# Convolution and layer-norm phase order by way of DRAM, Toeplitz weights on GpSimd, and a third GLU block among the x loads

## The reference

```python
u = glu[..., :D_CONV] * jax.nn.sigmoid(glu[..., D_CONV:])      # 1024 channels
uc = jnp.concatenate([u_past, u], axis=1)
y = lax.conv_general_dilated(uc, w_dw[:, None, :], ...) + b_dw  # depthwise, 31 taps along the sequence
y = jax.nn.silu(layer_norm(y, ln_g, ln_b))                      # over the 1024 channels
conv_out = y @ w_pw + b_pw
```

## Time and profile before

| | |
|---|---|
| median of 3 runs | 2202.6 us (2202.15 to 2210.67) |
| profiled execution, device time | 2203.41 us |
| its span, slowest core (6) | 2201.9 us; all cores 2185.9 to 2201.9 |
| TensorE busy | 2026.9 us, 92% |
| VectorE, ScalarE, GpSimd busy | 740.7, 441.7, 133.4 us |
| DMA, mean | 106 GB/s |

### The profile page before, as it was taken

How to read it: one execution, slowest core, us unless ns; L and a number is a source line. 1 busy time by engine, 2 the same in 40 slices (tenths; PEclk the granted TensorE clock), 3 DMA queues, 4 the chain that set the end, 5 groups by cost and what they waited for, 6 DMA issues and landing times.

```text
span 2201.9 us, 35215 instructions; the slowest of 8 cores (2185.9 to 2201.9 us)
## 1 busy us (share of the span) xinstructions
PE 2026.9 (92%) x13348; PEld 1266.4 (58%) x13348; DVE 740.7 (34%) x1185; ACT 441.7 (20%) x814; POOL 133.4 (6%) x253
## 2 busy tenths in 40 slices
PE   4667876499999999999999999999999999999997
PEld 3445543266555456666678865565565665655653
DVE  3445553222232232222223414414324224234126
ACT  4323434333222331111102310000000000000113
POOL 0000005500000000000000000000000000000000
PEclk9778777799999999999999999999999999999999
DMA  9244343323966868796374455584674643542423
GB/s 242 45 106 89 89 76 77 65 76 92 156 130 126 138 112 188 114 179 120 62 140 118 77 101 100 93 153 85 107 139 84 108 91 70 98 82 47 89 41 153
DMA packets 58459, 234.42 MB, mean 106 GB/s; under 512 B 13773, under 2 KB 32317, under 8 KB 43037
## 3 DMA queue, kind: packets, MB, share of 16 engines
q0 software_dynamic: 32080, 139.94, 38.1%
q1 hardware_dynamic: 26214, 92.23, 15.1%
HBM read 349.99 MB, written 59.99 MB: 186 GB/s over the span
## 4 chain that ended last, share of the span: by engine, by line
PE 84%; DMA 5%; DVE 3%; ACT 3%; issue 2%; POOL 2%; SPq 1%; DVEq 0%; ACTq 0%; POOLq 0%
PE ps L125 84%; DVE arena L125 3%; DMA arena<-xext 3%; ACT arena L125 2%; DMA arena<-arena 2%; POOL arena L142 2%; SPq L142 1%; ACT L125 0%; DMA y<-arena 0%; DVEq L85 0%; ACTq L85 0%; SPq L85 0%; POOLq L85 0%
## 5 line engine op out<-in xcount | busy, mean ns | idle before, releaser
L125 PE MATMUL ps<-arena 128*128 128x512 bf16 (+10 forms) x13348 | 2026.9, 320 | 161.4 <-DVE arena L125 122.7
L125 PEld LDWEIGHTS ps<-arena 128*128 128x128 bf16 (+2 forms) x13348 | 1266.4, 102 | 921.5 <-issue 206.9
L125 DVE TENSOR_TENSOR arena<-ps,arena 128x512 f32<-128x512 f32 (+5 forms) x729 | 412.7, 569 | 966.2 <-PE ps L125 710.5
L125 ACT ACTIVATE arena<-ps 128x348 f32<-128x348 f32 (+3 forms) x284 | 132.4, 476 | 1073.3 <-PE ps L125 1072.0
L125 ACT ACTIVATE arena<-arena 128x1 f32<-128x1 f32 (+7 forms) x183 | 124.1, 689 | 251.1 <-DVE arena L125 193.5
L125 DVE TENSOR_TENSOR arena<-arena 128x128 bf16<-128x128 f32 (+10 forms) x219 | 144.0, 661 | 36.4 <-ACT arena L125 18.2
L125 DVE SCALAR_TENSOR_TENSOR arena<-ps,arena 128x348 f32<-128x348 f32 (+4 forms) x74 | 46.7, 631 | 293.4 <-PE ps L125 291.1
L125 ACT COPY arena<-ps 128x512 bf16<-128x512 bf16 (+7 forms) x151 | 91.7, 621 | 129.8 <-PE ps L125 112.5
L125 DVE SCALAR_TENSOR_TENSOR arena<-arena 128x2048 bf16<-128x2048 f32 (+5 forms) x36 | 79.2, 2201 | 74.8 <-ACT arena L125 68.7
L125 ACT CAST arena<-ps 128x384 bf16<-128x384 f32 x72 | 36.9, 513 | 183.0 <-PE ps L125 181.4
L142 POOL DMA_DIRECT2D arena<-arena x128 | 63.3, 499 | 39.6 <-ACT arena L125 35.5
(11 more groups left out here) (18 smaller groups left out, 44.7 us busy)
## 6 DMA issues: line engine op xcount, KB each, us to landing
arena<-wgu POOLq DMA_DIRECT2D x44, 1024.0 KB, 8.3
arena<-wgate POOLq DMA_DIRECT2D x16, 1408.0 KB, 18.2
arena<-w_down POOLq DMA_DIRECT2D x11, 2048.0 KB, 27.1
arena<-xext SPq DMA_DIRECT2D x19, 1024.0 KB
arena<-wqkv POOLq DMA_DIRECT2D x9, 2048.0 KB, 17.8
kso<-ck SPq DMA_DIRECT2D x16, 1022.0 KB
vso<-cv SPq DMA_DIRECT2D x16, 1022.0 KB
arena<-wglu POOLq DMA_DIRECT2D x8, 1024.0 KB, 11.5
```

The costliest lines, as they stand in the source:

```text
L125: self.q[eng].append(lambda e, meth=meth, a=a, kw=kw, s=s: getattr(e, meth)(*a, **kw).then_inc(s, 1))
```

## The change

1. `glu_end` writes its block to a DRAM tensor `u_scr` with one DMA and reads it back in the other order with four, one for each f. They stay on SyncE's queue; the reads wait for the write.
2. The Toeplitz builds leave `glu_end` and VectorE: `tbuild(n)` does them on GpSimd, for blocks 0 and 1 in `consts`, for n + 2 at the end of `conv(n)`, each q with a key of its own.
3. `ln_n` is split in `ln_norm` and `ln_silu`. The Silu writes bf16 over its own fp32 operand; one DMA writes the block to `c_scr` in DRAM and four read it into `cT`, all on SyncE's queue instead of GpSimd's. `ln_step` does the norm of block i and the Silu of block i - 1, at steps 4 to 7 and twice at each of k and v steps 0 and 1, once at 2.
4. Blocks 0, 1 and 2 of GLU run among the first tiles, one third of one block behind a tile. A fourth weight slot and a third `uph` buffer come with it. Halo tiles 0 and 1 are loaded at tile 2. `conv(0)` follows directly.
5. In the loop over blocks 3 to 7 the norm of the next halo tile is issued right behind the transposes of the last one, and `conv(n - 1)` stands between the second and the last third of block n.
6. Weight loads move with the slots: GLU 4 and 5 behind `conv(0)`, GLU 6 and the q weights behind block 4, GLU 7 behind block 5, and the k weights in halves behind blocks 6 and 7.
7. `conv_last` moves from step 0 to step 1, `ln_sample` to 2 and `ln_mean` to 3; in group 2 the sample projection moves from k and v step 1 to 2.

```diff
+    u_d = nc.dram_tensor("u_scr", [8, 128, 1056], BF16, kind="Internal").ap()
+    c_d = nc.dram_tensor("c_scr", [8, 128, 1024], BF16, kind="Internal").ap()
...
-        GLUW = (0, 2048, 8192)
+        GLUW = (0, 2048, 8192, 10240)
+        GLUS = (0, 1, 2, 3, 0, 1, 0, 1)
...
+        after('pool', XBK[4])
+        glu_load(2)
...
         def glu_end(n):
-            for q in range(4):
-                for f in range(4):
-                    S.dma('sp', uP[ui][32 * f:32 * f + 32, q, :], uph[ui][32 * q:32 * q + 32, f, :], reads=[pk], writes=['%s_%d%d' % (Pk, q, f)])
+            S.dma('sp', u_d[n], uph[hi][:, :, :].rearrange("p f m -> p (f m)"), reads=[pk], writes=['ud%d' % n])
+            for f in range(4):
+                S.dma('sp', uP[ui][32 * f:32 * f + 32, :, :], u_d[n].rearrange("(q c) (f m) -> f c q m", q=4, f=4)[f], reads=['ud%d' % n], writes=['%s_%d' % (Pk, f)])
...
+        def tbuild(n):
             w4n = w4[:, 144 * n:144 * n + 144]
             for q in range(4):
-                S.op('dve', lambda e: e.tensor_tensor(out=v3(tpw[ui][q], 36), ...
+                S.op('pool', lambda e: e.tensor_tensor(out=v3(tpw[n % 2][q], 36), ...
...
-        GLU_AT = {2: 0, 5: 1, 9: 2}
+        GLU_AT = {2: ((0, 0),), 3: ((1, 0),), 5: ((0, 1),), 6: ((1, 1),), 7: ((2, 0),), 8: ((2, 1),), 9: ((0, 2), (1, 2), (2, 2))}
...
+            for n, part in GLU_AT.get(ti, ()):
+                glu(n, part)
+                if part == 2 and n < 2:
+                    glu_end(n)
+                    conv_out(n)
+        conv(0)
+        glu_end(2)
+        glu_load(4)
+        glu_load(5)
...
+        def halo_T():
+            tile_T(ht[0])
+            ht[0] += 1
+            if ht[0] < len(tiles):
+                halo_norm()
+        halo_norm()
+        for n in range(3, 8):
             glu(n, 0)
             conv_out(n - 1)
+            if n == 3:
+                conv(1)
+            if n % 2 == 0:
+                halo_T()
             glu(n, 1)
+            if n % 2 == 1:
+                halo_T()
+            conv(n - 1)
             glu(n, 2)
             glu_end(n)
+            if n % 2 == 0:
+                halo_T()
...
+            if n == 4:
+                glu_load(6)
+                qkv_load(2, 'q')
+            if n == 5:
+                glu_load(7)
+            if n == 6:
+                qkv_load(2, 'k', (0,))
+            if n == 7:
+                qkv_load(2, 'k', (1,))
...
+        yB = ab(YR, 8192).rearrange("p (n q m) -> p n q m", n=8, q=4)
+        def ln_silu(n):
+            for q in range(4):
+                S.op('act', lambda e: e.activation(out=yB[:, n, q, 0:256], in_=yP[:, n, q, :], func=AF.Silu, ...), [yk, 'vecP'], [yk])
+            S.dma('sp', c_d[n].rearrange("p (q m) -> p q m", q=4), yB[:, n, :, 0:256], reads=[yk], writes=['cd%d' % n])
+            for q in range(4):
+                S.dma('sp', mkap(cT[32 * q:32 * q + 32, n, 0:1], [[260, 4], [1, 256]]), c_d[n].rearrange("(f c) (q m) -> q c f m", f=4, q=4)[q], reads=['cd%d' % n], writes=['cT%d_%d' % (n, q)])
...
+        def ln_step():
+            i = lctr[0]
+            lctr[0] += 1
+            if i < 8:
+                ln_norm(i)
+            if 0 < i <= 8:
+                ln_silu(i - 1)
...
-                    S.alias(['num', 'den'], ['y%d' % n for n in range(8)] + ['yS'])
+                if g == 2 and n < 3:
+                    ln_step()
+                    if n == 2:
+                        S.alias(['num', 'den'], ['y%d' % n for n in range(8)] + ['yS'])
```

More of the change, by code:

```diff
@@ L352, in build_program @@
         hb = ab(o, 1024); o += 1024
-        uph = [v3(ab(o + 528 * i, 528), 4) for i in range(2)]; o += 1056
+        uph = [v3(ab(o + 528 * i, 528), 4) for i in range(2)] + [v3(ab(YR + 4096, 528), 4)]; o += 1056
+        UP0 = o
         uP = [v3(ab(o + 528 * i, 528), 4) for i in range(2)]; o += 1056
@@ L430, in qkv_w, with qkv_load @@
             return v3(wreg(QKVW[c], 4096), 16), 'W' + c
-        def qkv_load(g, c):
-            S.dma('pool', wreg(QKVW[c], 4096), wqkv[3 * g + 'qkv'.index(c)], writes=['W' + c])
+        def qkv_load(g, c, halves=(0, 1)):
+            src = wqkv[3 * g + 'qkv'.index(c)]
+            if halves == (0, 1):
+                S.dma('pool', wreg(QKVW[c], 4096), src, writes=['W' + c, 'W' + c + 'b'])
+                return
+            for h in halves:
+                S.dma('pool', wreg(QKVW[c] + 2048 * h, 2048), src[:, 4096 * h:4096 * h + 4096], writes=['W' + c + ('b' if h else '')])
         nctr = [0]
@@ L495, in consts @@
             S.dma('pool', dmask, dmask_d, writes=['dmask'])
+            glu_load(3)
             S.dma('pool', mb[:, :, :], masks_d, writes=['mb'])
+            for i in range(2):
+                tbuild(i)
             for i in range(2):
@@ L578, in conv @@
                         S.op('pe', lambda e: e.matmul(PS[bk][:, 256 * q2:256 * q2 + 256], lhsT=tpw[ui][q][:, 128 * s:128 * s + 128], rhs=uP[ui][:, q, s:s + 256], start=(s == 0), stop=(s == 8)),
-                             [tk] + ['%s_%d%d' % (Pk, q, f) for f in range(4)], [PSK[bk]])
+                             ['tp%d_%d' % (ui, q)] + ['%s_%d' % (Pk, f) for f in range(4)], [PSK[bk]])
                 yk = 'y%d' % n
@@ L614, in build_program @@
                 tile_load(ti + 8)
-            if ti == 1:
-                after('pool', XBK[5])
-                glu_load(2)
+            if ti == 2:
+                S.alias(['uph2'], [XBK[2]])
+                after('pool', XBK[7])
                 consts()
+                after('sp', XBK[0])
+                for t in range(2):
+                    tile_load(NFIRST + t)
             if ti == 7:
@@ L631, in build_program @@
+        S.alias(['y%d' % n for n in range(4)] + ['yS'], XBK[0:4])
+        conv(0)
+        glu_end(2)
+        S.alias(['y%d' % n for n in range(4, 8)], XBK[0:4] + ['uph2'])
         glu_load(4)
+        glu_load(5)
         S.dma('sp', convs_d[:, 0:26, :], state_d.rearrange("(s r) c -> s r c", r=30)[:, 4:30, :], writes=['convs'])
-        S.alias(['y%d' % n for n in range(8)] + ['yS'], XBK[0:4])
-        ht = NFIRST
-        for n in range(2, 8):
-            tile_norm(ht)
+        ht = [NFIRST]
@@ L669, in conv_last @@
             conv(7)
-            S.alias(['Wv'], ['tp0', 'tp1'])
+            S.alias(['Wv', 'Wvb'], ['tp%d_%d' % (i, q) for i in range(2) for q in range(4)])
             qkv_load(2, 'v')
@@ L709, in build_program @@
         late = late1 + late2
-        S.alias(first, xh_keys + ['hb_b'])
+        S.alias(first, xh_keys)
         kst = [af(gbc_off, 512), af(gbc_off + 512, 512)]
@@ L1150, in group @@
                     tab_load(0, 8, 9)
-                if n == 1:
+                if n == (2 if g == 2 else 1):
                     sample_qkv(g)
@@ L1154, in group @@
                         qkv_load(g - 1, 'q')
-                if n == 2:
+                if n == (3 if g == 2 else 2):
                     sample_T(g)
```

132 lines of the change are left out of this document (53 added, 79 removed).

## The result

| | before | after |
|---|---|---|
| median | 2202.4 us (4 runs) | 2152.3 us (4 runs) |
| profiled execution, span of the slowest core | 2201.9 us (core 6) | 2150.0 us (core 2) |
| TensorE's clock, mean by core | 0.953 to 0.964 | 0.971 to 0.974 |
| VectorE, ScalarE, GpSimd busy | 740.7, 441.7, 133.4 us | 731.0, 451.9, 142.9 us |

The ratio is 0.9765, with a 95% interval of 0.9731 to 0.9798: 50 us less, where 88 were forecast. The time lies at the very upper end of the range (2080 to 2152), and the forecast itself is 38 us off. The question is where 37 of the 88 us went.

What follows compares the result with a forecast made beforehand. TensorE was taken as the bound, with gain only in the first 436.6 us: 95 + 24.4 + 137 + 92 = 348, 88 us less, the rest unchanged; 2113.4 us span, 2114 device time, range 2080 to 2152.

Steps and rivals of the forecast that it cites:

- C: Stage to 436.6 us before (group 2 q projections, layer norm, first three k and v blocks): forecast 92 us against 139.6.
- A: Opening stage, x loads with the first GLU parts: forecast to end at 95 us instead of 88.5.
- B1: Stage after the x loads, until 151.0 us before, where GLU block 2 is done: forecast 24.4 us, ending at 119.4.
- B2: GLU blocks 3 to 7 with their convolutions: forecast 137 us, ending at 256; before it took 146.
- convolution 4: Behind GLU block 4: reads held until the GLU and 2 MB q loads end, 14 to 15 us of new wait.
- the 5 for the clock: After the convolution 4 wait: 5 us more, some 30 matmuls at twice 0.157 us because of the lower granted clock.
- second rival: GpSimd's builds stop VectorE as they run: 3 to 5 us in each of 5 blocks, 8 in A; 2135 to 2145; chance 0.17.
- the last term: End of C: first write of num waits until all eight channel blocks have left to DRAM; 3 us of TensorE wait.
- third rival: SP bounds C: write and read legs take 8 us instead of 5.7, 18 us more on first num; 2132; chance 0.08.
- first rival: Short reads are not held by big loads, so convolution 4 doesn't wait: 20 to 25 us less, 2092; chance 0.2.
- fifth: DRAM trip takes as long as the 16 copies, order alone works: 10 us more in five blocks, 2165; chance 0.05.
- fourth: Slower than before: 32 GpSimd builds in a row set the pace, from 9.4 us each; 2285 at 12 us; chance 0.02.

## Why the prediction was right or wrong

**What bounds the kernel, and where the gain can come from**: right. What is behind the sample projection was carried over as 1765.3 us and measures 1764.9 without the wait. (The sum for C before, "56 us of work", has two k and v blocks where the stretch has three: 63. The forecast doesn't use it.)

**A**, 97.9 for 95. The chain per tile takes 8.4 us from table load to transposes, as forecast (its addends make 8.0 and 8.2, not 8.2 and 8.4). VectorE's scaling beside the builds takes 4.22 us instead of 2.35, one of the costs for which 3 us were taken.

**B1**, 26.9 for 24.4: right within 2.5 us.

**B2**, 148.3 for 137. The step that failed is the sentence "behind blocks 2 and 3 there is no load in flight or it has ended". GLU loads 4 and 5 are issued behind convolution 0 and were in flight when block 2's trip left; with the 9 us by which the builds had delayed it, block 2 cost 13.6 us where nothing was set. In terms of the sum: 13.6 for this, 0.6 for convolution 4 (15.6 for 15), 4.0 for 5 in front of convolutions 5 and 6, 4.4 of small waits where nothing was set, and TensorE busy 110.7 us for 117 (its work and the 5 for the clock); that makes the 11.3. The wait in front of convolution 4 was right in place and size and half right in its cause: that a small transfer lands at about the load's end, as read from the earlier trace rows, held, but it was the write that fell under it. I had given the write a chance to slip in, because it is of few long rows. No write followed here that left behind a load of 2 MB landed in under 10 us.

**The second rival**, GpSimd stops VectorE, is true as a mechanism, and the runs with the scaling on ScalarE and with late builds on VectorE show it. Its price is not 3 to 5 us in five blocks but nearly all in block 2, where two blocks' builds follow one another with two loads issued in between; elsewhere pairs of VectorE steps take 2.6 to 5.2 us instead of 1.4 and TensorE hardly notices. The Trainium skill's SBUF — State Buffer, section "SBUF: two separate sides", names steps with two SBUF inputs or in a 2-port mode as those that exclude GpSimd. For steps of 128x512 with two inputs the trace agrees: one that meets a build ends 0.5 us behind it, and so takes up to 2.6 us instead of 0.7. The step of 9.01 us is more than that: it has one SBUF input beside a scalar, and it was held over four GpSimd operations in a row, not one. Why it got no turn between them, as the others did, stays open.

**GpSimd's build** was taken at 2.4 us and measures 2.285. The Trainium skill's figure (GPSIMD Engine Reference, section 3.1) led to an estimate of 2.5, and the trace bears it out to a tenth.

**C**. Up to the sample projection it took 87.9 us for 88.9, with the rope tables' wait at 9.5 for 8. The failed step is the last term, "3 us" for `num`, which measures 24.1. It was the write's landing, 14 us behind TensorE's arrival, less 11 us of projections that TensorE still had to do. Measured: the write landed at 383.4, 22.6 us behind the end of the sample projection (360.8), TensorE had 7.0 us of work left (to 367.84), and it went on only 8.5 us after the landing: 22.6 - 7.0 + 8.5 = 24.1. So all three parts were off, and the largest two are these.

First, the landing. I worked out the time of the last write from 5.7 us a block, without a load. A block takes 4.5 in quiet, but the last write lay 16.1 instead of 2.6 us, 13.5 more, because the next group's q load, which the diff shows at k and v step 2, was out by then, with the cache copy for a smaller part. I had the rule in B2 and did not apply it in C.

Second, I priced the wait as if TensorE went on when the write lands. Between the landing and TensorE's next matmul (391.95) stand ScalarE's six copies and VectorE's sample steps, all queued behind the waiting instruction. The trace of before shows this price at the same place, in its chain of waits:

```profile
425.20 2.90 DMA arena<-arena
428.56 0.58 ACT arena L125
...
436.61 63.46 PE ps L125 x364
```

The last small copy of layer norm lands at 428.1, ScalarE then has its sample copies, and TensorE goes on at 436.6, 8.5 us later as well. The wait was thus not quite new: in the kernel before, ScalarE waited at this place for the small buffers.

**The third rival** put SyncE as the bound of C at 18 us more; the wait's 21 us more came where it said, by way of `num`, but only in part by its mechanism: from the first write to the eighth (324.02 to 367.36) a block took 6.2 us, for 5.7 forecast and 8 in the rival. The run with all writes first shows the order's part and the load's only together. It had 0.08, and its place together with the second rival's lock is what happened. My range, 2152 at its upper end, was built from one rival at a time; the lower end of the second (2135, by its own addends 2137) with the third's 18 us on top is 2153 to 2155. That this is near the measured time, and that the time falls on the range's end, is luck: neither rival's cost came about as it was worked out. By the signs that the prediction itself had set, it was wrong: a VectorE operation beside a build was longer than before (9.01 us for 0.25), and `num` waited over 10 us. A third sign, no VectorE wait of 6 us in blocks 3 to 7, failed with the 6.44 us at 143.27.

**The first rival** (short reads pass beside loads) is out: in the run with the scaling on ScalarE the reads themselves lay beside the loads until these had landed. The **fifth** said that the trip takes as long as the 16 copies; it doesn't. But what it said beside that, that the order alone works, is nearly so: with the 16 copies in the new order the kernel is only 2 to 6 us slower. The **fourth** needed builds of 9.4 us.

## What to carry to other kernels

Put a transfer that TensorE will soon wait for, and the weight loads of another queue, into an order of their own: here a load that waited for the small transfer cost 3.3 to 7.0 us of TensorE's time, and a small transfer behind a load lay for about the load's whole remaining time. For every instruction that gets a new wait, list what stands behind it on its engine and price the wait up to the moment at which the bound engine goes on, not up to the landing. And when a step is moved off a busy engine, ask what it holds up there: here 24 builds on GpSimd instead of VectorE gained nothing. Last, when two profiles are cut into stretches, check that the cuts lie behind the same instruction; here a cut at the longest wait was one step further on and hid 7 us of one stretch in another.

## What the runs showed of the hardware

A write of 264 KB from SyncE's queue landed in 2.1 to 2.6 us with no weight load out, in 7.9 beside two 1 MB loads issued 9.6 us earlier, in 10.6 beside the rest of a 2 MB load, and in 16.6 beside 3 MB. Where such a write or read was held, it landed between 5.7 us before and 2.2 us after the load did, over the runs shown, and with a 1 MB cache copy ahead of it in SyncE's queue 3.7 to 6.2 us after. With such a copy ahead of it and no weight load out, a write of 256 KB lay 5.8 to 8.0 us. A 32-column VectorE step took 9.01 us beside four GpSimd operations, and ended with the last of them; on ScalarE the same step took 0.35 us at the same place. A VectorE step of 128x512 with two SBUF inputs took up to 2.6 us instead of 0.71 where it met such an operation, and the operation 2.56 instead of 2.12.
